# Expert blocks of a hybrid decoder layer: token rows and middle rows turned by VectorE in 32x32 squares instead of by TensorE

## The reference, cut to what matters

```
expert_ids, gates = top-1 group of 8, then top-2 of its 8 experts     # 2112 tokens x 2 = 4224 rows over 64 experts
for each block of up to 128 rows of one expert e:
    xb = x[rows of the block]                      # 128 x 1024, x = RMSNorm(h)
    mid = silu(xb @ w_gate[e]) * (xb @ w_up[e])    # 1024 -> 256
    y   = mid @ w_down[e]                          # 256 -> 1024
y of each token is summed with its gates and added to h, then a last RMSNorm
```

## Time and profile before

| | |
|---|---|
| median of 3 runs | 2602.05 us (2592.71 to 2602.96) |
| the profiled execution | 2603.91 us, span 2602.2 us |
| PE busy, mean granted clock over the span | 90%, 0.952 |
| the stretch from 1907.6 to 2367.9 us (steady expert blocks) | PE busy throughout, DMA 364 GB/s |
| first expert weights issued, last scatter issued | 1715.05 us, 2516.31 us |

### The profile page before, as it was taken

One profiled execution on the slowest core, in us unless ns is written; L12 is line 12 of the kernel. 1 busy time (PEld: TensorE's weight loads), 2 busy tenths in 40 slices (PEclk: granted clock), 3 DMA queues, 4 the chain that ended last, 5 costly groups with the idle time before them and its releaser, 6 DMA issues. The chain is left out here.

```text
span 2602.2 us, 36339 instructions
## 1 busy us (share of the span) xinstructions
PE 2333.2 (90%) x13208; PEld 1339.2 (51%) x13208; DVE 1027.2 (39%) x1762; ACT 707.5 (27%) x1825; POOL 456.6 (18%) x632
## 2 busy tenths in 40 slices
PE   7999999999968999999999999849999999999940
PEld 3454454533546666666667666524444444444420
DVE  4415234224226554456656656341111211112128
ACT  3203122012025544345444554201111111111112
POOL 1010100100200011200131311212222212212235
PEclk9999999999978999899999999969999999999975
DMA  8041230400373112121122111167999999999967
GB/s 283 26 134 33 57 103 9 131 11 11 97 226 76 56 61 88 52 65 56 56 79 88 56 56 61 60 250 297 367 362 361 363 369 370 361 362 361 354 249 314
DMA packets 165971, 440.35 MB, mean 169 GB/s; under 512 B 36961, under 2 KB 78169, under 8 KB 141225
## 3 DMA queue, kind: packets, MB, share of 16 engines
q1 hardware_dynamic: 139351, 350.38, 37.7%
q0 software_dynamic: 20640, 70.29, 6.8%
q10 hardware_dynamic: 5842, 17.80, 1.8%
HBM read 345.11 MB, written 94.80 MB: 169 GB/s over the span
## 5 line engine op out<-in xcount | busy, mean ns | idle before, releaser
L867 PE MATMUL p_ps<-p_xt,p_w 128*128 128x512 f32 x1088 | 476.7, 597 | 0.5 <-DVE p_xt L698 0.5
L3056 PE MATMUL p_ps<-p_w_arena,p_x_arena 128*128 128x512 f32 x1024 | 446.6, 594 | 0.0
L867 PEld LDWEIGHTS p_ps<-p_xt,p_w 128*128 128x128 f32 x1088 | 205.2, 191 | 255.2 <-issue 250.0
L3056 PEld LDWEIGHTS p_ps<-p_w_arena,p_x_arena 128*128 128x128 f32 x1024 | 195.5, 191 | 245.4 <-issue 245.4
L2426 PE MATMUL p_ps<-p_w_out,p_mixt 128*128 128x512 f32 x544 | 252.5, 609 | 0.0
L3072 PE MATMUL p_ps<-p_w_arena,p_y_arena 128*128 128x512 f32 x512 | 236.0, 604 | 0.0
L2978 DVE SCALAR_TENSOR_TENSOR p_y_arena<-p_y_arena,p_ps 128x256 f32<-128x256 f32 x64 | 27.0, 422 | 459.9 <-ACT p_y_arena L2863 358.2
L2426 PEld LDWEIGHTS p_ps<-p_w_out,p_mixt 128*128 128x128 f32 x544 | 99.6, 193 | 105.8 <-issue 103.7
L876 PE MATMUL p_ps<-p_w,p_xt 128*128 128x144 f32 (+1 forms) x512 | 146.6, 440 | 0.0
L2807 POOL DMA_INDIRECT s_y<-p_y_arena,p_home x66 | 65.0, 985 | 462.3 <-PE p_ps L3043 266.6
L3072 PEld LDWEIGHTS p_ps<-p_w_arena,p_y_arena 128*128 128x128 f32 x512 | 93.1, 192 | 98.2 <-issue 93.0
(11 more groups left out here) (415 smaller groups left out, 3254.1 us busy)
## 6 DMA issues: line engine op xcount, KB each, us to landing
p_w_arena<-in_w_exp_gate SPq DMA_DIRECT2D x64, 1024.0 KB, 7.9
p_w_arena<-in_w_exp_up SPq DMA_DIRECT2D x64, 1024.0 KB, 11.1
p_w_arena<-in_w_exp_down SPq DMA_DIRECT2D x64, 1024.0 KB, 10.6
p_w_arena<-s_y SPq DMA_DIRECT2D x16, 1024.0 KB, 13.3
p_x<-in_x_prompt SPq DMA_DIRECT2D x30, 512.0 KB, 4.8
p_w<-in_w_in SPq DMA_DIRECT2D x4, 2048.0 KB, 15.5
p_spread<-s_roots SPq DMA_DIRECT2D x16, 512.0 KB, 7.1
s_kv<-p_us SPq DMA_DIRECT2D x32, 256.0 KB, 2.3
```

The source lines that it names most:

```text
L867: ins = mm(ps[:, job % 4, :], w[:, c, at:at + P], xt[s % 2][:, c, :], start=(c == 0), stop=(c == KC - 1))
L3056: t = mm(ps[:, 2 + b, :], xt[b][:, c, :], w_gu[bw][:, :, c, :], start=(c == 0), stop=(c == KC - 1))
```

## The change

The token rows are no longer turned by PE. `hn` is written to DRAM with its 1024 columns in another order, each row is gathered as four pieces of 1 KB from a table of 4 x 2112 quarter rows, and partition 32q+r of piece g gets quarter q of the token in lane 32g+r. One DVE instruction (`turn_x`) then turns all 32 x 32 squares of the tile. For this the rows of the gate and up weights must lie on other partitions, so each 1 MB of gate or up weights is loaded as four transfers of 32 partitions. `mid` is turned by 16 DVE instructions of 32 partitions x 64 (`turn_mid`). Lanes without a token are now marked with an index out of bounds and are skipped by gathers and scatters. PE runs gate and up of block j, then down of block j-1. At the start, PE spreads the token numbers over the partitions (4 small matmuls) and DVE has six more small operations. In `gather_listed` the list of rows is read five times (once as before, four times by quarters) and eleven small operations prepare the indices.

```diff
@@ load_weights (SP)
-                    sp.dma_start(w_gu[b][:, t].rearrange("p c f -> p (c f)"),
-                                 src[bass.ds(e, 1)].rearrange("o (p c) f -> p (o c f)", p=P)).then_inc(arrived[b], 16)
+                    for q in range(4):
+                        sp.dma_start(w_gu[b][32 * q:32 * q + 32, t].rearrange("a c f -> a (c f)"),
+                                     src[bass.ds(e, 1)].rearrange("o (a q c) f -> q a (o c f)", q=4, c=KC)[q]).then_inc(arrived[b], 16)
@@ fetch_rows (POOL)
-                pool.indirect_dma_start(out=x[b], out_offset=None, in_=S["hn"],
-                                        in_offset=bass.IndirectOffsetOnAxis(ap=slot[b][:, 0:1], axis=0)
-                                        ).then_inc(x_in[b], 16)
+                for g in range(4):
+                    apart(pool, on["slots_ready"], 1)
+                    pool.indirect_dma_start(out=x[b][:, 256 * g:256 * g + 256], out_offset=None,
+                                            in_=S["hn"].rearrange("t (q k) -> (t q) k", q=4),
+                                            in_offset=bass.IndirectOffsetOnAxis(ap=slot[b][:, g:g + 1], axis=0),
+                                            bounds_check=4 * NTOK - 1, oob_is_err=False).then_inc(x_in[b], 16)
...
@@ gather_listed (POOL)
+                    for k in range(4):
+                        pool.dma_start(raw[n][32 * k:32 * k + 32, 1:5],
+                                       S["ids"][bass.ds(q, 1)].rearrange("o (g b) -> b (o g)", g=4)).then_inc(raw_in[n], 16)
...
@@ DVE
+            def turn_x(j, b, bx, x_count):
+                dve.wait_ge(x_in[bx], x_count)
+                dve.wait_ge(gu_done.sem, gu_done.back(j, 2))
+                nc.vector.transpose(xt[b].rearrange("p c (g r) -> p g c r", g=4), x[bx].rearrange("p (g c a) -> p g c a", g=4, c=KC)
+                                    ).then_inc(xt_ready.sem, 1)
...
+            def turn_mid(j, b):
+                dve.wait_ge(mid_ready.sem, mid_ready.all(j))
+                dve.wait_ge(down_done.sem, down_done.back(j, 2))
+                for q in range(4):
+                    for g in range(4):
+                        t = nc.vector.transpose(midt[b][32 * q:32 * q + 32, :, 32 * g:32 * g + 32],
+                                                mid[b][32 * g:32 * g + 32].rearrange("p (q a c) -> p q c a", q=4, c=FC)[:, q])
+                t.then_inc(midt_ready.sem, 1)
@@ PE
-                        turn(j + 2, b, (bw + 2) % R, 4 * i + (16 if half_ == 0 else 32))
...
+            def blocks(i, first=0):
+                for n in range(first, R):
+                    gate_up(i + n, n % 2, n, 16 * i + 64)
+                    down(i + n - 1, (n + 1) % 2, (n - 1) % R, 4 * i + (16 if n else 0))
```

More of the change, by code:

```diff
@@ L20 @@
 NT = SEQ // P
+ABSENT = 1 << 20
 DB, DT = 8, 8
@@ new lines, in blocks @@
+            def blocks(i, first=0):
+                for n in range(first, R):
+                    j, b = i + n, n % 2
+                    gate(j, b)
+                    evacuate_y(j - 1, 1 - b, 8 * i + 16 * ((n + 1) // 2))
+                    turn_mid(j, b)
+                    turn_x(j + 2, b, (n + 2) % R, 16 * i + (64 if n < 2 else 128))
+            turn_x(0, 0, 0, 64)
+            turn_x(1, 1, 1, 64)
+            gate(0, 0)
+            turn_mid(0, 0)
+            turn_x(2, 0, 2, 64)
+            blocks(0, 1)
@@ L3076, in _, with gate_up @@
-            turn(0, 0, 0, 16)
-            turn(1, 1, 1, 16)
-            with pe.Fori(0, NE - R, R) as i:
+            pe.wait_ge(on["sel_ready"], 1)
+            pe.wait_ge(on["token_ready"], 1)
+            for g in range(4):
+                t = mm(ps[:, 4, g * NE:(g + 1) * NE], sel[:, g].rearrange("p q b -> p (q b)"), token, start=True, stop=True)
+            t.then_inc(on["spread"], 1)
+            def gate_up(j, b, bw, arrived):
+                pe.wait_ge(xt_ready.sem, xt_ready.all(j))
+                pe.wait_ge(mid_ready.sem, mid_ready.back(j, 2))
+                pe.wait_ge(gate_in[bw], arrived)
+                pe.wait_ge(up_in[bw], arrived)
+                for c in range(KC):
+                    t = mm(ps[:, 2 + b, :], xt[b][:, c, :], w_gu[bw][:, :, c, :], start=(c == 0), stop=(c == KC - 1))
+                t.then_inc(gu_done.sem, 1)
@@ new lines, in down @@
+            def down(j, b, bw, arrived):
+                pe.wait_ge(midt_ready.sem, midt_ready.all(j))
+                pe.wait_ge(down_in[bw], arrived)
+                for n in two:
+                    pe.wait_ge(y_act.sem if n else y_vec.sem, y_vec.back(j, 2))
+                    for c in range(FC):
+                        t = mm(ps[:, n if b else 5 + n, :], midt[b][:, c, :], w_dn[bw][:, c, n * 512:(n + 1) * 512],
+                               start=(c == 0), stop=(c == FC - 1))
+                    t.then_inc(down_done.sem, 1)
@@ L3079, in _, with blocks @@
+            def blocks(i, first=0):
+                for n in range(first, R):
+                    gate_up(i + n, n % 2, n, 16 * i + 64)
+                    down(i + n - 1, (n + 1) % 2, (n - 1) % R, 4 * i + (16 if n else 0))
+            gate_up(0, 0, 0, 64)
+            blocks(0, 1)
+            with pe.Fori(R, NE - R, R) as i:
                 blocks(i)
@@ L3082, in _ @@
                 blocks(i)
+            down(total - 1, 1, R - 1, total * 4)
 def scratch(nc):
```

226 lines of the change are left out of this document (97 added, 129 removed).

## The result

The changed kernel takes 2966.74 us (median of 4 runs, 2961.51 to 2974.84), the kernel before 2600.78 us beside it: ratio 1.142, 95% interval 1.138 to 1.145. It is slower, as forecast, but by 366 us instead of 153, and outside the range. The profiled execution took 2966.44 us, 362.5 more than the one of before.

A forecast was written before the change was run, and what follows sets the result against it. The prediction took the DMA engines, slowed by narrow weight loads, as the new bound instead of PE: 2603.9 + 73 + 8 + 72 = 2757, stated as 2755 us. The range was 2620 to 2840 us (2690 to 2835 for this case alone).

The forecast's parts named there:

- term 1: Up to the scatter of block 55: DMA-bound blocks of 13.4 us; +73 us (+36 to +116).
- term 2: The start: later indices and four-piece gathers leave the load queue empty; +8 us (0 to +20).
- Term 3: POOL's last eight turns: 9 us more each for added reads, gathers and small operations; +72 us (+52 to +98).
- DVE at nothing: Steady blocks: DVE's 5.9 to 6.7 us a block hide inside PE's 10.3 us and cost nothing.
- Rival (a): Weight loads: small transfers run at full width's rate, PE stays the bound at 10.3 us; 2633 us, chance 0.16.
- Rival (b): As Rival (a), but POOL's last turns pay for their instructions out of their waits; 2589 us, chance 0.09.
- Rival (c): Weight loads: a quarter of the partitions gives a quarter of the rate, 104 GB/s; 3,300 us, chance 0.05.

The follow-up runs named there:

- e2: The kernel before, with gate and up loaded as two transfers of 64 partitions; 2869.86 us.
- e1: The kernel before, with gate and up of each block loaded as four transfers of 32 partitions; 2802.71 us.
- e12: The changed kernel with no lane skipped, neither by gathers nor by scatters; 2893.3 us.
- e4: The changed kernel with gate and up weights loaded as full-width transfers of 128 partitions and `hn`'s columns reordered to match; 2618.14 us, ratio 1.008.
- e11: e1 with the scatters' lanes without a token skipped, gathers still whole rows; 2915.0 us.
- e6: e1 with each transfer taking runs of 8 KB, one in every 32 KB of DRAM, as in the changed kernel; 2829.72 us.

## Why the prediction was right and wrong

**The mechanism held.** Narrow loads make the DMA engines the bound, PE waits for gate and up in every block, and this outweighs PE's gain. The first loads ran at 222 GB/s with the engines busy throughout, where 208 was taken; slices of 1 us with down weights show up to 426 GB/s, so 408 for those was about right as long as nothing else was in flight. The rule of the Trainium skill, page "SBUF — State Buffer", section "Door 1: The DMA port swizzle (why `[64,N]` ≈ `[32,N]`)", that 32 partitions get no more than 64 (at most about 218 GB/s), agrees with 222 within 2% for loads by themselves. In a mix it does not hold to the letter: e2's halves took 2869.86 us and e1's quarters 2802.71. What the same page says in section "Can I just issue two DMAs to hit both halves?", that such transfers don't add up, agrees with e1, where pieces on both halves stood in the queue and the loss stayed.

**The step that failed is the block time of term 1.** The sentence was "a block costs 12.7 us (all hidden) to 14.2 us (nothing hidden). I take 13.4", with skipped lanes counted as 0.54 MB at 364 GB/s. Two assumptions stood in it: that rows and down weights keep full rate beside narrow loads, so that parts add up, and that skipped lanes can only save. The window of the steady blocks shows 225 GB/s over everything, though a third of the weights' bytes are full-width. The second assumption is wrong in sign: skipping costs 73 us (e12), where it was to save. For whole rows the prediction's own prices give 12.7 + 2.9 = 15.6 us a block, and e1 and e12 measure 15.0 and 15.7; taking the lanes away was to bring this to 14.2, and it brought 16.6. The first assumption does not hold either: in e1, 4 KB of rows take 0.22 us of an engine instead of 0.16, which is 1.0 us more a block for 256 rows on 16 engines. That e1 still came under 15.6 is in part luck, since its weights took less than their price. The upper end of 14.2 was therefore no bound: "nothing hidden" is not the worst case when traffic slows other traffic.

**Term 1 and term 2 in numbers.** Loads began at 1711.78 (3.3 us earlier). In the stall the DMA engines had a share of 0.28 over 30 us, so the queue stood empty for 21.6 us, where 8 were taken and 20 was the upper end: the chain of small writes, each waiting for the one before, ran from 1764.00 to 1817.10, 53 us instead of 35 before the change, so that the gather of block 4 came at 1820.69 instead of 1810, with PE idle for 35.69 us. Besides, the prediction let the loads go on behind gate and up of block 4. They go on only at 1840.50, behind down of block 3, which the change has put after it. The rest of the way to 2691.68, by the prediction's own sum, is 1711.8 + 38 + 21.6 + 10.1 + 11 + 53 x 17.0, so that 53 blocks took 3.6 us each more than taken: 190 us. With 13.6 us of term 2 and less 3.3 us that is the 200 us by which +281 exceeds +81.

**Term 3 was right in its range**: +79.8 against +72 (52 to 98), and two deviations partly cancel. Unloaded turns went from 9.3 to 17.0 us, 7.7 more where 9 were taken. Loaded ones grew by more, up to 31.7 us: there POOL waited 13.01, 16.27, 17.18 and 6.78 us for the list, 20 us more in all than the 6.12, 11.56, 8.02 and 7.64 of before, and the sum had this only in its upper end. With full-width loads (e4) it was +52, the lower end.

**DVE at nothing was right** for the steady blocks: 16 turnings at 0.24 us and one of 1.24 us (0.2 and 1.2 to 2.1 had been taken), and DVE is busy for 6.5 us of a block. The gathers' start from block to block was 6.06 us against 6.4.

**Rival (a)** is out by the 222 GB/s of the first loads and by e1. It had PE's part right: the scatter of block 55 at 2368 us without the price of narrow loads, 2372.54 in e4. **Rival (b)** (turns paid from waits) did not come: a turn grew by 6.5 us even in e4, more than its 5.4. **Rival (c)**, 104 GB/s, is excluded by the 222.

What stays open: why skipped lanes slow all traffic beside narrow loads, and why a mix with loads of 64 partitions is slower than one with loads of 32.

## What to carry to other kernels

A layout that needs the weights in strips of partitions must be paid from the DMA side: before accepting it, look for an order of the small operand (here `hn`'s columns) that leaves the big one in one full-width transfer; that was worth 349 us here. Where a resource near its limit gets slower traffic, a sum of parts at their own rates is no upper bound: it fitted with whole rows (15.6 against 15.0 and 15.7 us a block) and failed with skipped lanes (14.2 against 16.6). And when a change lengthens a chain on one engine, look at what that chain holds at both ends of the loop. With full-width loads the change lost 0.8%, and with the ends mended as well it gained 2.2%; the ends alone gave the kernel before 0.8%.

## What the runs showed of the hardware that was not expected

- Skipping 62 of 128 lanes of a scatter by an index out of bounds made the kernel with narrow loads 112 us slower (e11 against e1), at the same busy share of the DMA engines; with full-width loads PE waits for nothing with it (e4). A skipped lane still leaves a packet of 4 bytes.
- Beside loads of 32 partitions, 4 KB of rows take an engine 0.22 us instead of 0.16 (e1), and 0.27 where lanes are skipped (e11).
- Gate and up in two transfers of 64 partitions are slower than in four of 32: 2869.86 against 2802.71 us, one run each.
- Four transfers of 256 KB over 128 partitions cost no more than one of 1 MB: 2604.27 us, 365 GB/s.
- Spread addresses, runs of 8 KB out of every 32 KB, cost 27 us in 64 blocks (e6 against e1, one run each).
